# The gated mLSTM branch's gates and values as one product from seven half products

## The reference

```python
qk_a = silu(causal_conv(qk_a, conv_w, conv_b))            # branch A: 4 heads of 256
ha   = rms_norm(mlstm_scan(qa, ka, va, i_pre, log_f), mlstm_norm_g)
y_a  = ha * sigmoid(o_a) * silu(z_a)
y_b  = dsa_attention(qb, kb, vb, ...) * silu(z_b)         # branch B: 8 heads of 128, top-k keys
y_m  = memory_attention(qm, km, vm) * silu(z_m)           # branch M: 4 heads of 256, 256 memory tokens
merged = g[0]*(y_a @ w_branch[0]) + g[1]*(y_b @ w_branch[1]) + g[2]*(y_m @ w_branch[2])   # g = sigmoid(gate)
x = x + merged @ w_out
```

## Time and profile before

| what | us |
|---|---|
| median of three executions | 1009.39 (1008.74 to 1009.84) |
| the profiled execution, its own time | 1011.33 |
| its span, first to last instruction | 1009.0 |
| PE busy in the span | 1000.1 |
| DVE, ACT, POOL busy | 588.4, 458.8, 102.1 |
| one head of A, from spread to spread | 65.0 |

### The profile page before, as it was taken

The page is one execution under the profiler, slowest core; times in us unless marked ns, Lnnn a source line. Parts: engine busy times, 40 slices in busy tenths (PEclk is TensorE's granted clock), DMA queues, the critical chain, the costliest instruction groups (busy, mean ns, idle before and its releaser), DMA issues.

```text
span 1009.0 us, 13840 instructions
## 1 busy us (share of the span) xinstructions
PE 1000.1 (99%) x5109; PEld 864.5 (86%) x5109; DVE 588.4 (58%) x997; ACT 458.8 (45%) x707; POOL 102.1 (10%) x74
## 2 busy tenths in 40 slices
PE   8999999999999999999999999999999999999998
PEld 6878888888998998989988887988979888888887
DVE  4878988688565465465467648455484334523352
ACT  6777544436454444454454744525435322322230
POOL 1000822121011011011010000000100000000000
PEclk9999999999999999999999999999999999999999
DMA  7723222212233232332321131321312422334221
GB/s 236 265 84 125 84 84 73 63 53 74 64 94 93 62 94 71 85 94 62 105 95 52 63 126 42 112 76 62 126 39 80 130 86 83 95 114 164 100 101 53
DMA packets 108570, 94.92 MB, mean 94 GB/s; under 512 B 3984, under 2 KB 98548, under 8 KB 108532
## 3 DMA queue, kind: packets, MB, share of 16 engines
q1 hardware_dynamic: 108516, 94.40, 30.2%
q10 hardware_dynamic: 16, 0.00, 0.0%
HBM read 92.30 MB, written 2.10 MB: 94 GB/s over the span
## 4 chain that ended last, share of the span: by engine, by line
PE 94%; DVE 3%; ACT 1%; issue 1%; DMA 1%; SPq 0%; ACTq 0%; DVEq 0%
PE proj L483 80%; PE att L790 2%; PE att L851 1%; PE att L808 1%; PE att L752 1%; DVE a_atl L1883 1%; PE proj L646 1%; PE att L798 1%; PE att L730 1%; PE att L779 1%; DVE w_lo L1375 1%; DMA w_raw<-w_mem_kv_in 1%; DVE score L1625 1%; PE att L864 0%; PE att L865 0%
## 5 line engine op out<-in xcount | busy, mean ns | idle before, releaser
L1375 DVE TENSOR_TENSOR w_lo<-w_raw,w_hi 128x2048 fp32r<-128x2048 f32 (+2 forms) x91 | 186.5, 2050 | 209.3 <-ACT w_hi L930 207.6
L483 PE MATMUL proj<-hT_hi,w_hi 128*128 128x512 f32 x640 | 250.7, 392 | 0.0
L483 PE MATMUL proj<-hT_hi,w_lo 128*128 128x512 f32 x640 | 249.4, 390 | 0.0
L483 PE MATMUL proj<-hT_lo,w_hi 128*128 128x512 f32 x640 | 249.3, 390 | 0.0
L930 ACT ACTIVATE w_hi<-w_raw 128x2048 fp32r<-128x2048 f32 (+2 forms) x91 | 153.6, 1688 | 189.0 <-PE proj L483 186.8
L483 PEld LDWEIGHTS proj<-hT_hi,w_hi 128*128 128x128 f32 x640 | 120.2, 188 | 27.1 <-issue 3.0
L483 PEld LDWEIGHTS proj<-hT_hi,w_lo 128*128 128x128 f32 x640 | 120.1, 188 | 25.2
L483 PEld LDWEIGHTS proj<-hT_lo,w_hi 128*128 128x128 f32 x640 | 120.3, 188 | 24.0
L483 PE MATMUL proj<-w_hi,hT_hi 128*128 128x384 f32 (+2 forms) x408 | 133.3, 327 | 0.5
L483 PE MATMUL proj<-w_hi,hT_lo 128*128 128x384 f32 (+2 forms) x408 | 131.5, 322 | 0.0
L483 PE MATMUL proj<-w_lo,hT_hi 128*128 128x384 f32 (+2 forms) x408 | 131.4, 322 | 0.0
(11 more groups left out here) (300 smaller groups left out, 1408.8 us busy)
## 6 DMA issues: line engine op xcount, KB each, us to landing
w_raw<-w_in_in SPq DMA_DIRECT2D x72, 512.0 KB, 3.9
w_raw<-w_in_in SPq DMA_DIRECT2D x80, 256.0 KB, 3.2
w_raw<-w_branch_in SPq DMA_DIRECT2D x16, 512.0 KB, 4.9
w_raw<-w_mem_kv_in SPq DMA_DIRECT2D x5, 1024.0 KB, 5.2
yF<-x_in SPq DMA_DIRECT2D x8, 512.0 KB, 7.1
w_raw<-w_branch_in SPq DMA_DIRECT2D x16, 256.0 KB, 3.5
w_raw<-w_out_in SPq DMA_DIRECT2D x4, 1024.0 KB, 5.0
w_raw<-w_mem_kv_in SPq DMA_DIRECT2D x4, 512.0 KB, 6.4
```

The source lines that it names most:

```text
L483: ins = mm(ps, lhs[a](k, k0), rhs[b](k, k0), start=(first and k == 0 and j == 0), stop=(last and k == KH - 1 and j == 2))
L1375: V.tensor_tensor(w_lo[:, kh, :, 0:n], w_raw[:, kh, :, 0:n], w_hi[:, kh, :, 0:n].bitcast(F32), ALU.subtract).then_inc(w_lo_done, 1)
```

## The change

The operands of the gate, z and value projections of a head are put together: h is seen as 2 x 2 blocks (256 tokens x 512 rows), and the 1024 x 768 weight as 2 x 2 blocks (512 rows x 384 columns; left: 256 columns of the output gate and 128 of z, right: the other 128 of z and 256 of the values). The product of two 2 x 2 block matrices is made from 7 block products (Strassen in Winograd's form) instead of 8. The 4 sums of blocks of h are made once, on POOL, the 4 sums of weight blocks in every head, on POOL. Each of the 7 products is 2 token tiles x 4 row tiles x 3 matmuls of 384 columns. Partial results are saved by ACT (`unit_save`), added by DVE (`unit_add`) or left to add up in PSUM. A head's weights now are 11 operands (4 half panels of queries and keys, 7 for the products), each split by ACT and DVE into one of three slots.

The seven products need room: a half of `w_raw`, parts of `w_hi` and `w_lo`, the arena and most of `merged`. The merge panels of the sparse branch (GB) are therefore moved ahead of branch A, and `merged` is written to DRAM and read back after the last head. The gates are applied before the turn instead of after it. Several semaphores are joined into counters (`gate_steps`, `a_norm_steps` and others), with the same points of waiting.

```diff
-AS = _plan.take(3 * A_HEADS, 5 * A_HEADS, (3 * A_HEADS,) * 4)
 GB = _plan.take(4, 8, (4,) * 4)
+AS = _plan.take(0, 0, (A_HEADS,) * 4)
@@ SP
+            def load_head(h, first, last):
+                left = [(h * A_HD + C_OA, A_HD), (h * A_HD + C_ZA, P)]
+                right = [(h * A_HD + (C_ZA + P), P), (h * A_HD + C_VA, A_HD)]
...
+                raw_half(raw_f, "f", h * A_HD + C_KA, 1)
+                raw_block(raw_a, "a", left, 0)
+                raw_block(raw_b, "b", right, 0)
+                if first:
+                    sp.wait_ge(g_merged, 8)
+                    sp.dma_start(merged_kept, merged[:, :]).then_inc(kept, 16)
+                    sp.wait_ge(kept, 16)
+                raw_block(raw_c, "c", left, 1)
+                raw_block(raw_d, "d", right, 1)
@@ PE
+            gated(GB, 0, (0, 1, 2, 3), y_split(2), {1: [lambda: b_score(g)], 3: [lambda: b_turn_p(g)],
+                                                    5: [lambda: b_values(g)]})
+            def unit_product(h, i, lhs, to, start, before):
...
+                pe.wait_ge(op_low, h * OPERANDS + (n + 1))
+                for t in range(2):
+                    pe.wait_ge(*before(t))
+                    for k in range(KH):
+                        for j, (a, b) in enumerate(((0, 0), (0, 1), (1, 0))):
+                            ins = mm(to[t][:, 0:UNIT_N], lhs[a](k, t), w[b][:, k, :], ...)
+            def unit(h, first):
+                unit_product(h, 0, h_block(0, 0), last_pair, True, ...)
+                unit_product(h, 1, h_block(KH, 0), first_pair, True, lambda t: (bank_empty[t], h + (AS[2][t] + 1)))
+                a_spread_max(h, first)
+                pe.wait_ge(s_low, 4)
+                unit_product(h, 2, h_sum(1), second_pair, True, lambda t: (bank_empty[2 + t], h + (AS[2][2 + t] + 1)))
+                unit_product(h, 3, h_sum(2), last_pair, False, lambda t: (u_saved, h * 6 + (t + 1)))
+                unit_product(h, 4, h_sum(3), second_pair, False, lambda t: (u_saved, h * 6 + (t + 3)))
+                unit_product(h, 5, h_sum(0), last_pair, False, lambda t: (u_saved, h * 6 + (t + 5)))
+                a_scores(h)
+                unit_product(h, 6, h_block(KH, HALF_T), last_pair, False, lambda t: (u_added, h * 6 + (t + 5)))
+            gated(GA, 0, (0, 1, 2, 3), y_split(3), {1.5: [lambda: a_numerators(g)], 4: [lambda: a_turn_h(g)]})
@@ ACT
+            split_hi(GB[0], 1, GB[1] + 2, 512, (2, BS[2][2] + 2 * B_HEADS))
+            split_y(yF, range(0, 4))
+            b_exps(B_HEADS - 1)
+                elif n in (3, 5):
+                    act.wait_ge(op_used, h * 2 + (1 if n == 3 else 2))
...
+                elif n == 6:
+                    act.wait_ge(proj_done[3], h + (AS[2][3] + 1))
@@ DVE
+            split_lo(GB[0], 1, 512)
+            split_y(yF, 2, range(0, 4))
+            b_maxes(B_HEADS - 1)
...
+            b_finish(B_HEADS - 1)
+            split_y(yF, 2, range(KT - 1, KT))
@@ POOL
+            pool.wait_ge(b_y, B_HEADS)
+            for f, (k0, t0) in enumerate(((0, HALF_T), (KH, HALF_T), (0, 0), (KH, 0))):
+                hi, lo = h_part(k0, t0)
+                ins = G.tensor_tensor(s_full[f], hi, lo, ALU.add)
...
+            def weight_sums(h):
+                pool.wait_ge(raw_landed["b"], h * 32 + 32)
+                pool.wait_ge(op_low, h * OPERANDS + 5)
+                G.tensor_tensor(raw_a, raw_b, raw_a, ALU.subtract).then_inc(t_done, 1)
+                pool.wait_ge(raw_landed["d"], h * 32 + 32)
+                pool.wait_ge(op_low, h * OPERANDS + 7)
+                G.tensor_tensor(raw_a, raw_d, raw_a, ALU.subtract).then_inc(t_done, 1)
+                G.tensor_tensor(raw_b, raw_d, raw_b, ALU.subtract).then_inc(t_done, 1)
+                pool.wait_ge(t_done, h * 4 + 2)
+                G.tensor_tensor(raw_c, raw_c, raw_a, ALU.subtract).then_inc(t_done, 1)
```

More of the change, by code:

```diff
@@ L164, in hybrid_block @@
         negmask = sb("negmask", [P, off(TT)])
+        negmask_at = nc.sbuf_base - 4 * off(TT)
         score = sb("score", [P, off(TT)])
@@ L454, in _ @@
+            sp.wait_ge(op_low, last + OPERANDS)
+            sp.wait_ge(u_done, 2 * PRODUCTS * A_HEADS)
+            sp.wait_ge(u_added, 6 * A_HEADS)
+            sp.wait_ge(a_half, 2 * A_HEADS - 1)
+            sp.dma_start(merged[:, :], merged_kept).then_inc(kept_back, 16)
+            with sp.Fori(1, 4) as j:
                 load(j + GA[0], [(wi, j * 256 + C_GATE, 256), (wb[0], j * 256, 256)])
@@ L831, in _, with gated, a_spread_max @@
             turns_of(pe, None, B_HEADS, 0, b_body)
-            def a_spread_max(h):
-                if isinstance(h, int) and h == 0:
+            def gated(sec, j, order, before, hooks=None):
+                panel(j + sec[0], [(b, j + sec[2][b], w_as_lhs(b * P), all_tokens(hT if b < 2 else yT), S,
+                                    before if b == 2 else None) for b in order], hooks)
+            g = B_HEADS - 1
+            gated(GB, 0, (0, 1, 2, 3), y_split(2), {1: [lambda: b_score(g)], 3: [lambda: b_turn_p(g)],
+                                                    5: [lambda: b_values(g)]})
+            with pe.Fori(1, 4) as j:
+                gated(GB, j, (2, 3, 0, 1), None)
+            def a_spread_max(h, first):
+                pe.wait_ge(a_params, h + 1)
+                if first:
                     pe.wait_ge(b_y, B_HEADS)
@@ L1248, in _, with gates @@
             turns_of(act, steps, B_HEADS, 0, b_body)
+            def gates(sec, j, n, to):
+                for b in range(2):
+                    act.wait_ge(proj_done[b], j + (sec[2][b] + 1))
+                    if not (isinstance(n, int) and n == 0):
+                        act.wait_ge(g_merged, n * 2 + (b - 1))
+                    A_(to[b], banks[b][:, :], ACT.Sigmoid).then_inc(bank_empty[b], 1)
+            split_hi(GB[0], 1, GB[1] + 2, 512, (2, BS[2][2] + 2 * B_HEADS))
+            split_y(yF, range(0, 4))
@@ new lines, in _, with raw_of, operand @@
+            with act.Fori(1, 3) as j:
+                gb_body(GB, j, j, j * 2 + (GB[1] + 4), gb_sig)
+                gates(GB, j, j, gb_sig)
+            gb_body(GB, 3, 3, None, gb_sig)
+            def raw_of(n, first):
+                if n == 1 and first:
+                    return raw_f_first
+                return (raw_e, raw_f, raw_e, raw_f, raw_a, raw_c, raw_a, raw_a, raw_d, raw_b, raw_c)[n]
+            def operand(op, n):
+                return op[SLOT[n]][:, 0:D].rearrange("p (h n) -> p h n", h=2) if n < 4 else op[SLOT[n]]
@@ L1298, in a_body @@
                     A_(dst, src, ACT.Copy).then_inc(a_qkhigh, 1)
+                operand_high(9, h)
+                unit_save(h, 3, last_half, u_second, 2)
                 a_weights(h)
[L1300 to L1306 removed]
@@ new lines, in _, with raw_of, operand @@
+            b_finish(B_HEADS - 1)
+            split_y(yF, 2, range(KT - 1, KT))
+            gb_merge(GB, 0, 0, gb_sig)
+            with dve.Fori(1, 3) as j:
+                gb_body(GB, j, j, gb_sig)
+            split_lo(GB[0] + 3, 1, 512)
+            def raw_of(n, first):
+                if n == 1 and first:
+                    return raw_f_first
+                return (raw_e, raw_f, raw_e, raw_f, raw_a, raw_c, raw_a, raw_a, raw_d, raw_b, raw_c)[n]
+            def operand(op, n):
+                return op[SLOT[n]][:, 0:D].rearrange("p (h n) -> p h n", h=2) if n < 4 else op[SLOT[n]]
```

697 lines of the change are left out of this document (443 added, 254 removed).

## The result

The changed kernel takes 1001.09 us (median of four executions, 1000.06 to 1002.79) against 1009.07 us before; the ratio is 0.9922, with a 95% interval of 0.9905 to 0.9939. That is 8.0 us faster; forecast were 1002.4 us, with a gain of 7.05 us. On the chip of the last experiments the two stood at 1001.98 and 1009.08 us, 7.1 apart.

What follows compares the result with a forecast made beforehand. PE was taken as the bound. Terms 17.2 - 2.25 - 3.6 - 3.4 - 0.9 = 7.05 us, off the profiled 1011.33, gave 1004.3; with the median 1.94 lower, 1002.4 us, range 996 to 1008.5.

Steps and rivals of the forecast that it cites:

- The products (17.2 us): PE in all heads: seven products replace the gate, z and values panels, saving 4.3 us a head, 17.2 in all.
- The later heads (2.25 us): Three later heads: POOL's sums hold back DVE's splits, so PE waits 0.75 us each before the sixth product.
- The steps of the list: Reckoned DVE and POOL times in a later head: tenth operand ready at 48.8 us, sixth product due at 48.05.
- The first head (3.6 us): First head: operand six loads only after `merged` is written out; PE waits 3.6 us, bounds 1.6 and 7.
- The tail (3.4 us): First GB panel: 2.35 us before the last sparse head's transposes and 1.05 for the last tile of `yF`.
- The end (0.9 us): First GA panel: DVE's splits and normalisation make the turn late by 0.9 us, bounds 0 and 2.5.
- The first, no meeting of DVE and POOL: All parts: DVE and POOL hardly meet, so the heads' stalls vanish, the first keeping 1.6 us; 997 us, chance 0.18.
- rows 8 to 11: Earlier profile rows: DVE splits begun at 468.78 and 707.94 stood until POOL's operations ended at 469.33 and 709.89.
- The second, POOL first: Four heads: POOL goes first when both wait, 1.55 us more in each; 1008.6 us, chance 0.11.
- The third, the way out: First head: writing out `merged` takes far beyond 7.1 us; at a third of the pace 1016 us; chance 0.07.
- The fourth, convolutions held: Heads: POOL's sums also hold back convolutions, about 8 us a head; some 1030 us, chance 0.03.

Runs made afterwards that it cites:

- eight products: Changed kernel with the last of the seven products made twice in each head: 1018.83 us, ratio to before 1.0088.
- the repeated one: The changed kernel run and profiled once more, unedited, on the chip of the later runs: 1001.98 us.
- without the late block: Changed kernel with `merged` saved in two pieces, so that row blocks load into it before the first head's queries end: 998.22 us.
- without POOL's sums: Changed kernel with the four sums of weight blocks of each head cut to 16 of 1536 columns: 998.62 us.
- four moves of single instructions or transfers: Changed kernel with yF splits first in the tail, h sums later, `merged` saved in pieces and tenth operand split first: 993.03 us.
- the kernel with the wait of 6.94 us: Changed kernel with `merged` written out twice before the two row blocks are loaded into it: 1006.23 us.

## Why the prediction was right, and where it wasn't

**The products (17.2 us).** Right. 0.1733 us per matmul where 0.1731 was taken, 4.36 us less a head without the wait, where 4.3 was said; eight products put back 16.9 us. By the formula of the Trainium skill (TensorE: Matmul & The Clock Gate, Back-to-back issue gap) 384 columns take 0.1625 us, and the estimate from it was 3.9; the measured distances decide for the earlier trace rows.

**The later heads (2.25 us).** The mechanism is right, the size was off: 0.5 us. DVE and POOL take turns as described. In one later head:

```profile
709.27 2.32 DVE L2092 SCALAR_TENSOR_TENSOR negmask<-proj,small,negmask 128x511 f32<-128x511 f32 x3
...
714.58 2.60 DVE L2078 TENSOR_TENSOR w_lo<-w_raw,w_hi 128x1536 fp32r<-128x1536 f32 x1
...
717.70 4.46 DVE L2078 TENSOR_TENSOR op_lo<-merged,op_hi 128x1536 fp32r<-128x1536 f32 x1
...
725.43 1.74 DVE L2078 TENSOR_TENSOR w_lo<-w_raw,w_hi 128x1536 fp32r<-128x1536 f32 x1
```

```profile
708.59 3.51 POOL L2323 TENSOR_TENSOR w_raw<-merged,w_raw 128x1536 f32<-128x1536 f32 x1 [3.98 <-DVE w_lo L2078]
712.06 3.50 POOL L2324 TENSOR_TENSOR w_raw<-merged,w_raw 128x1536 f32<-128x1536 f32 x1
715.51 5.04 POOL L2326 TENSOR_TENSOR merged<-merged,w_raw 128x1536 f32<-128x1536 f32 x1
```

The split of 714.58 stands until POOL's third sum ends at 715.56; then it runs, and now POOL's fourth, begun at 715.51, takes 5.04 us instead of 3.50: it waits for the split to end at 717.2, and holds the next split (4.46) until 720.5. The steps of the list come within half a microsecond. In this head, which starts at 678.70, the tenth operand is ready after 48.5 us (at 727.2), where I had 48.8, and the sixth product is due after 48.4, where I had 48.05; it starts at 727.30. A wait of 0.75 us that is a difference of two sums over 48 us had no right to two decimals: 0.3 less on one side and 0.4 more on the other leave hardly anything, and the 0.17 measured is mostly the time from DVE's end to PE's start. This agrees with the rule of the Trainium skill (SBUF — State Buffer, Who interferes with whom) for the two-input splits; the convolutions, which read PSUM, kept their 2.3 us for three (709.27, while POOL's second sum ran from 708.59 to 712.10).

**The first head (3.6 us).** 3.4 us in this profile and 4.1 in the repeated one, by the mechanism named: without the late block 0.9 is left, without POOL's sums 1.8. But it is not one wait before the sixth product, as reckoned, but five, the first (0.89) already before the second product. The parts differ too: the last of the weights ahead landed at 632.0 (issued at 624.79, 7.2 us), 13.2 us into the head and not 10.5; the way out ran partly beside them and landed 4.9 us later, not 7.1, and the block 5.2 behind it, not 4.4.

**The tail (3.4 us).** The waits were right, 1.9 + 0.4 + 1.2. The step that failed is one that I had put at nothing without a reason, the clock behind the wait: 1.45 us more in the profiled execution, and the like in about half of the executions. With that the term was 4.9 us.

**The end (0.9 us).** 0.7 before the turn as expected, and 0.45 before the first GA panel for its first weight half, which I had not costed.

**The sum.** 4 x 4.36 - 0.5 - 3.4 - 4.9 - 1.2 = 7.4 us, against 6.6 measured in the stretch. Behind each wait the second matmul starts about 0.1 us later than elsewhere; eight waits whose terms don't hold this yet (the last tile's, five in the first head, two at the end) make up the rest. That 7.05 us lies so near is partly luck: the two largest errors cancel, 1.75 us too much for the later heads and 1.5 too little for the tail. The medians' 8.0 us (7.1 on the other chip) is more than the stretch's 6.6; with executions 1 to 3 us apart, no run shows where the difference comes from.

**The rivals.** The first, no meeting of DVE and POOL, falls by the 4.46 us split and by the run without sums. (That rows 8 to 11 show the exclusion "to the hundredth" was too much: a split that stood until 469.33 and then took 1.76 us would have ended at 471.09, and it ended at 470.95.) The second, POOL first, falls by POOL's 5.04 us. The third, the way out, was the right path at the wrong price: 6.1 us for 2 MB more. The fourth, convolutions held, falls by 2.32 us for three of them beside a sum.

## What to carry to other kernels

An arithmetic saving shows in full only if the queues that prepare its operands keep their order: here 8 us came at once, and 9 more from four moves of single instructions or transfers. When something is moved away from in front of a late step, look who reads it before choosing where it goes; move what is read last. And count PE's waits of about 2 us at more than their length.

## What the runs showed of the hardware that was not expected

- After a wait of 1.92 us on PE the granted clock stood at its lower level for 3.4 us in four of seven profiles and, by the mean clock, in roughly half of the executions (17 of 31), and about 1.5 us were lost. In kernels without a longer wait there than 1.51 us it did so in none of 17; eight of these have the wait of 1.51 us. In the kernel with the wait of 6.94 us, which has the one of 1.92 too, the profile shows the low clock at both, and the mean clock of the five executions was 0.994 to 0.997.
- The exclusion between DVE and POOL alternates when both queues are full: a DVE split that waits goes next, though POOL's next sum follows with no gap, and that sum then stands for 1.5 us (5.04 us instead of 3.50).
- Writing 2 MB out of SBUF behind 2 MB of loads took 11.5 us from issue; a second 2 MB took 6.1 us more.
